# Attention layers of a two-block network: values weighted once per head slot, 256 columns, in place of once per query tile, 128 columns

## What is computed

```python
def _dilated_group(q, k, v, bias, window, dilation):
    ...
        logits = jnp.einsum('bqhd,bqkhd->bhqk', qb, kb, ...) * scale
        logits = logits + bias.astype(jnp.float32)[None, :, None, :]
        logits = jnp.where(valid[None, None], logits, NEG_INF)
        lse = jax.nn.logsumexp(logits, axis=-1)
        p = jnp.exp(logits - lse[..., None]).astype(vb.dtype)
        o = jnp.einsum('bhqk,bqkhd->bqhd', p, vb)
    ...
    wts = jax.nn.softmax(jnp.stack(lses, axis=0), axis=0)
    attn = jnp.einsum('gbsh,gbshd->bshd', wts, jnp.stack(outs, axis=0).astype(jnp.float32))
```

## Time and profile before

| | us |
|---|---|
| median of 3 runs | 1478.26 |
| lowest and highest | 1477.96, 1479.23 |
| profiled execution, its own time | 1477.93 |
| its span (first to last instruction) | 1476.1 |
| TensorE matmuls busy | 1463.0 (99%) |
| VectorE busy | 1131.1 (77%) |
| ScalarE busy | 801.4 (54%) |
| TensorE clock granted | 9 tenths or more (full) in each of 40 slices |

### The profile page before, as it was taken

One profiled execution on the slowest core, in us unless ns is written; L12 is line 12 of the kernel. 1 busy time (PEld: TensorE's weight loads), 2 busy tenths in 40 slices (PEclk: granted clock), 3 DMA queues, 4 the chain that ended last, 5 costly groups with the idle time before them and its releaser, 6 DMA issues.

```text
span 1476.1 us, 23650 instructions
## 1 busy us (share of the span) xinstructions
PE 1463.0 (99%) x10012; PEld 1311.9 (89%) x10012; DVE 1131.1 (77%) x1158; ACT 801.4 (54%) x931; POOL 470.2 (32%) x300
## 2 busy tenths in 40 slices
PE   9999999999999999999999999999999999999997
PEld 7889899888888889899888889998888899988886
DVE  7867776798787767776898667977997568789853
ACT  7444544665544444554666456356665446676642
POOL 3306200234698608001234744002444000134510
PEclk9999999999999999999999999999999999999999
DMA  8674455555556564466555444434554534355552
GB/s 288 228 222 175 143 172 176 196 181 190 185 206 250 182 246 143 143 252 240 186 186 200 158 162 168 140 119 172 195 180 182 188 130 161 143 194 179 191 186 79
DMA packets 48585, 269.93 MB, mean 183 GB/s; under 512 B 11488, under 2 KB 14816, under 8 KB 19552
## 3 DMA queue, kind: packets, MB, share of 16 engines
q1 hardware_dynamic: 48480, 268.43, 51.6%
HBM read 261.59 MB, written 6.82 MB: 182 GB/s over the span
## 4 chain that ended last, share of the span: by engine, by line
PE 96%; DVE 2%; ACT 1%; DMA 0%; issue 0%; SPq 0%; DVEq 0%; ACTq 0%
PE gemm L603 31%; PE gemm L576 23%; PE gemm L607 15%; PE aux L603 13%; PE aux L607 6%; PE aux L576 1%; PE aux L688 1%; ACT w_hi L1065 1%; PE aux L629 1%; DVE x_two L1518 0%; PE aux L810 0%; PE gemm L1006 0%; PE aux L690 0%; PE aux L665 0%; PE aux L678 0%; PE aux L670 0%
## 5 line engine op out<-in xcount | busy, mean ns | idle before, releaser
L1485 DVE TENSOR_TENSOR w_lo<-raw,w_hi 128x2048 fp32r<-128x2048 f32 (+3 forms) x244 | 588.4, 2415 | 131.8 <-ACT w_hi L1065 130.9
L1065 ACT ACTIVATE w_hi<-raw 128x2048 fp32r<-128x2048 f32 (+2 forms) x246 | 456.9, 1858 | 195.2 <-PE gemm L576 86.8
L603 PE MATMUL gemm<-x_two,w_hi 128*128 128x512 f32 x1184 | 373.4, 397 | 0.0
L607 PEld LDWEIGHTS gemm<-x_two,w_lo 128*128 128x128 f32 x1184 | 222.4, 188 | 52.6
L607 PE MATMUL gemm<-x_two,w_lo 128*128 128x256 f32 x1184 | 232.7, 278 | 0.0
L2215 POOL TENSOR_TENSOR tmp<-tmp 128x512 f32<-128x512 f32 (+1 forms) x29 | 43.8, 1510 | 466.9 <-ACT tmp L1092 453.3
L603 PEld LDWEIGHTS gemm<-x_two,w_hi 128*128 128x128 f32 x1184 | 180.4, 189 | 0.2
L2340 POOL TENSOR_TENSOR cv<-cv,rstd 128x512 f32<-128x512 f32 x44 | 112.0, 2545 | 210.6 <-ACT cv L1145 210.6
L603 PE MATMUL gemm<-y_two,w_hi 128*128 128x512 f32 x528 | 166.4, 396 | 0.0
L603 PE MATMUL aux<-x_two,w_hi 128*128 128x512 f32 x512 | 161.1, 396 | 1.0 <-DVE x_two L1518 1.0
L576 PE MATMUL gemm<-x_two,w_hi 128*128 128x256 f32 x672 | 123.2, 285 | 0.0
(11 more groups left out here) (388 smaller groups left out, 2675.5 us busy)
## 6 DMA issues: line engine op xcount, KB each, us to landing
raw<-in_weights SPq DMA_DIRECT2D x222, 1024.0 KB, 4.8
raw<-in_weights SPq DMA_DIRECT2D x16, 768.0 KB, 4.3
raw<-in_weights SPq DMA_DIRECT2D x8, 512.0 KB, 4.4
raw<-in_weights SPq DMA_DIRECT2D x4, 576.0 KB, 3.6
s_inputs<-s_made SPq DMA_DIRECT2D x1, 2048.0 KB, 8.9
s_outputs<-s_cw SPq DMA_DIRECT2D x1, 2048.0 KB, 10.8
s_v<-s_inputs SPq DMA_DIRECT2D x1, 2048.0 KB, 9.3
s_cw<-s_outputs SPq DMA_DIRECT2D x1, 2048.0 KB, 10.6
```

Source lines behind the costliest of these rows:

```text
L603: pe.matmul(dst[:, off:off + BANK], wh[:, wc, c0:c0 + P], both[:, xc, :, :], start=b.start and wc == 0, stop=b.stop and k + 2 == len(pairs ...
L607: mm = pe.matmul(dst[:, off:off + S], wl[:, wc, c0:c0 + P], both[:, xc, 0, :], start=False, stop=b.stop and k + 2 == len(pairs), skip_grou ...
L1065: me.give(act.activation(w_hi[i % SPL][:, 0:n], raw[i % RAW][:, 0:n], ACT.Copy), w_hi_ready)
L1485: me.give(v.tensor_tensor(w_lo[i % RAW][:, 0:n], raw[i % RAW][:, 0:n], w_hi[i % SPL][:, 0:n].bitcast(F32), ALU.subtract), w_lo_ready)
```

## The change

The values of a slot are weighted for both its query tiles at once. pt gets a place for each of the two tiles (ST = 2). `pv` is called with the slot, in the rounds 3, 5, 7 and 9, and in no other; it takes pt_ready twice. Its two products with va have 256 columns each, and four with vc of 64 columns follow, one for each class. ScalarE's copy and VectorE's subtraction take the 256 columns of a slot at once, in the same rounds. The copy to pt writes the tile's place, three pieces of 128. Products, sums and their order within an output are as before.

```diff
--- before.py
+++ after.py
@@ -266,7 +266,7 @@
         gate_p = tile("gate_p", r_gate, [P, DC, S])
         gate_a = tile("gate_a", r_gate + 8 * K, [P, DC, S])
         lg = tile("lg", r_att, [P, S + 2 * NC])
-        pt = tile("pt", r_att + 3 * K, [P, 3, P])
+        pt = tile("pt", r_att + 3 * K, [P, 3, ST, P])
         ao_h = tile("ao_h", r_att + 6 * K, [P, SLOTS, S], F32R)
         ao_l = tile("ao_l", r_att + 10 * K, [P, SLOTS, S], F32R)
 
@@ -678,17 +678,17 @@
                     mm = pe.transpose(A[:, 2 * BANK + k * P:2 * BANK + (k + 1) * P], lg[:, k * P:(k + 1) * P], ident)
                 me.give(mm, tr_ready)
 
-            def pv(u):
-                s, q = divmod(u, ST)
-                me.take(pt_ready)
-                if u:
+            def pv(s):
+                me.take(pt_ready, ST)
+                if s:
                     me.take(pv_read)
                 o, n, mm = 3 * BANK, slice(s * DH, (s + 1) * DH), None
                 for t in range(ST):
-                    pe.matmul(A[:, o:o + P], va[:, t, n], pt[:, t, :], start=t == 0, stop=False, skip_group_check=True)
-                for r in range(2):
-                    mm = pe.matmul(A[:, o + r * NC:o + (r + 1) * NC], vc[:, 2 * q + r, n], pt[:, 2, r * NC:(r + 1) * NC],
-                                   start=False, stop=r == 1, skip_group_check=True)
+                    pe.matmul(A[:, o:o + S], va[:, t, n], pt[:, t, :, :], start=t == 0, stop=False, skip_group_check=True)
+                for c in range(CLASS):
+                    q, r = divmod(c, 2)
+                    mm = pe.matmul(A[:, o + c * NC:o + (c + 1) * NC], vc[:, c, n], pt[:, 2, q, r * NC:(r + 1) * NC],
+                                   start=False, stop=c == CLASS - 1, skip_group_check=True)
                 me.give(mm, pv_ready)
 
             def table(k):
@@ -734,8 +734,8 @@
                         me.take(qkv_ready)
                     if j < 8:
                         scores(j)
-                    if 2 <= j:
-                        pv(j - 2)
+                    if j >= 3 and j % 2:
+                        pv((j - 3) // 2)
                     if 1 <= j < 9:
                         turn(j - 1)
                 me.take(scores_read)
@@ -1146,10 +1146,9 @@
                 y_half(PAIRS - 1)
                 then(first("down", n))
 
-            def pv_half(u):
-                s, q = divmod(u, ST)
+            def pv_half(s):
                 me.take(pv_ready)
-                me.give(act.activation(ao_h[:, s, q * P:(q + 1) * P], A[:, 3 * BANK:3 * BANK + P], ACT.Copy), pv_hi)
+                me.give(act.activation(ao_h[:, s, :], A[:, 3 * BANK:3 * BANK + S], ACT.Copy), pv_hi)
 
             def gate_of(j):
                 return (gate_p if j < 4 else gate_a)[:, 2 * (j % 4):2 * (j % 4) + 2, :]
@@ -1188,11 +1187,12 @@
                     split_next(ib)
                     if j >= 4:
                         gate(layer, j - 4)
-                    if 2 <= j:
-                        pv_half(j - 2)
+                    if j >= 3 and j % 2:
+                        pv_half((j - 3) // 2)
                     if 1 <= j < 9:
                         me.take(tr_ready)
-                        me.give(act.activation(pt.rearrange("p k n -> p (k n)"), A[:, 2 * BANK:2 * BANK + 3 * P], ACT.Copy),
+                        me.give(act.activation(pt[:, :, (j - 1) % ST, :],
+                                               A[:, 2 * BANK:2 * BANK + 3 * P].rearrange("p (k n) -> p k n", k=3), ACT.Copy),
                                 pt_ready)
                     if j < 8:
                         me.take(lg_ready)
@@ -1704,11 +1704,11 @@
                         lo(pl[:, :, :], tmp[:, :, :], ph[:, :, :])
                     else:
                         split_next(ib)
-                    if 2 <= j:
-                        s, q = divmod(j - 2, ST)
+                    if j >= 3 and j % 2:
+                        s = (j - 3) // 2
                         me.take(pv_hi)
-                        me.give(v.tensor_tensor(ao_l[:, s, q * P:(q + 1) * P], A[:, 3 * BANK:3 * BANK + P],
-                                                ao_h[:, s, q * P:(q + 1) * P].bitcast(F32), ALU.subtract), pv_read)
+                        me.give(v.tensor_tensor(ao_l[:, s, :], A[:, 3 * BANK:3 * BANK + S], ao_h[:, s, :].bitcast(F32),
+                                                ALU.subtract), pv_read)
                     if j < 8:
                         soft_a(j)
                     if j < 8:
```

## The result

The changed kernel takes 1486.3 us (median; 1484.24 to 1488.2) against 1478.17 us before: ratio 1.0053, 95% interval 1.0042 to 1.0065. It is slower by 8 us where 0.3 us faster was forecast.

The account below looks back on a forecast made before the run. TensorE was taken to bound the kernel. Per layer, three slots gain 0.03 us each, slot 3 loses 0.03, the pool gemm gains 0.09: 0.3 us over two layers, from 1478.26 to 1478.0 us; 8-in-10 range 1476.9 to 1479.3 us.

Parts of the forecast that it names:

- What bounds the kernel: Whole kernel: TensorE, busy 1463.0 of 1476.1 us; only its own time, or waits it is made to take, count.
- The rounds: Attention rounds 2 to 9: slots 0 to 2 gain 0.03 us each, slot 3 loses 0.03 us, per layer.
- The short rounds: Attention rounds 2, 4, 6, without values: 0.68 us from first head score to next gemm, 0.90 us shorter each.
- the long ones: Attention rounds 3, 5, 7, with a slot's values: 2.45 us from first head score to next gemm, 0.87 us more.
- the wide record: One 256-column f32 TensorE record of the values: 0.216 us, so four take 0.96 us, 0.42 us more.
- the weight load of the class values: Class values in long rounds: load-bound at 0.113 us each, no load saved; four more records cost 0.45 us.
- The pool gemm's wait: Pool gemm behind round 9, seventh chunk: TensorE's wait for VectorE's last subtraction goes, 0.09 us gained per layer.
- Beside TensorE: ScalarE's copy 0.38 us, VectorE's subtraction 0.41 us at 256 columns; sign: both engines with 1.2 us less each.
- Rival 1: Short rounds wait for the softmax, 0.6 us in rounds 2 and 4 of both layers: 1480.4 us; chance 0.05.
- Rival 3: Values' records at 256 columns take the 0.11 us of 128, eight slots gain 3.4 us: 1474.6 us; chance 0.02.
- the sum: Attention rounds and pool gemm: 0.15 us gained per layer, 0.3 us for two; from 0.5 slower to 0.8 faster.
- With 0.02 for what I don't see: Allowance for unseen effects in the odds for the whole kernel: faster 0.03, same 0.94, slower 0.03.

Follow-up runs that it names:

- after_again: The changed kernel run once more, unchanged, for a second trace: 1484.78 us, 1.0042 to the kernel before.
- before_m72: Kernel before, without the change, with 72 fewer TensorE instructions in the warm-up ahead of the first gemm: 1486.02 us, ratio 1.0048.
- after_p136: Changed kernel with 136 more TensorE instructions in the warm-up ahead of the first gemm: 1477.8 us, ratio 0.9997.
- after_slow72: Changed kernel with 72 TensorE instructions, 18 products of 128 columns at a gemm's pace, right ahead of the first burst: 1482.11 us, ratio 1.0026.
- after_split: Changed kernel, no padding, with groups 2 and 3 of the first burst moved between the two tiles of the gemm behind it: 1483.0 us, ratio 1.0029.
- after_mid72: Changed kernel with 72 TensorE instructions, 18 narrow products, put between the two bursts: 1484.77 us, ratio 1.0038.
- after_late72: Changed kernel with 72 TensorE instructions, 18 narrow products, put right ahead of the first burst: 1484.12 us, ratio 1.0040.
- after_m24: Changed kernel with 24 fewer TensorE instructions in the warm-up ahead of the first gemm: profiled execution 1480.04 us, the shortest of its six.
- after_m80: Changed kernel with 80 fewer TensorE instructions in the warm-up ahead of the first gemm; its measured time is not in the text given.

## Why the prediction was wrong

- *What bounds the kernel*: right. TensorE does, and each loss is one of its own.
- *The rounds*: right to 0.01 us. The short rounds took 0.69 us (0.68 forecast), the long ones 2.44 (2.45), the wide record 0.24 at most and 0.216 in series as in the earlier trace rows, and the weight load of the class values stayed the price of a 64-column record. Gained over both layers 0.25 us by the traces, 0.3 forecast.
- *The pool gemm's wait*: gone, 0.08 us a layer (0.09 forecast).
- *Beside TensorE*: ScalarE's wide copy took 0.375 us (0.38 forecast), VectorE's wide subtraction 0.419 us (0.41). So these two operations take 1.2 to 1.3 us less in all. The engines' busy time did not fall by that, as I had named as a sign: it is up by 2.6 us on VectorE, whose weight splits (w_lo) took 4.4 us more, and down by 0.3 us on ScalarE. I should have named the two lines in place of the totals.
- *Rival 1, late probabilities*: did not happen; no short round waits.
- *Rival 3, free columns*: did not happen; twice the columns took 0.216 us against 0.11.
- *The step that failed*: the sum put everything outside the attention rounds and the pool gemm at nothing, without a reason. "A difference of over 1 us in a stretch other than the attention rounds" stood at the end as a sign of error, but no term and no rival had a price for it; the runs showed 4.7 us at the two bursts from the place of TensorE's code, and 1.5 us near 1284 us. I counted the 32 records less as work saved and not as 72 instructions less of code. "With 0.02 for what I don't see" is where the result was. The trace of before had signs of it: the table of queues has q8 with 79 packets, TensorE's instructions divided by that are 257, and the burst's 512 instructions take 7.4 us, two pieces of code in a third of the time in which a gemm's code takes one (some 22 us). In it, too, 30 of the 79 code packets start right behind the close of a weight transfer. How much a late piece costs could not be read from it, since TensorE waited for none.

How the 8.1 us are made up: 3.3 us at the first burst, 1.4 us at the second and 1.5 us near 1284 us in the profiled execution, less 0.25 us in the rounds and 0.4 us of start on top, give its 6.3 us. That execution took 1484.24 us, the shortest of its kernel; the trace of after_again loses 4.8 us at the first burst, as its clock was low for 6.8 us there (before_m72 likewise, with 4.7 us). So the rest of the median is likely the same burst with a longer fall of the clock; the other executions have no trace that could show it.

A version that beats both did not come out: the change at a good place, after_p136, has 1477.8 us, and 0.9997 (0.9988 to 1.0007) is no difference that can be told.

## What to carry to other kernels

Count the instructions that a change takes from or adds to an engine, not only their time: behind it all code of that engine stands elsewhere against the ends of its pieces, and a kernel with dense bursts can lose several microseconds hundreds of microseconds further on. When a comparison shows a loss in a stretch that the edit does not touch and the wait is called "issue", shift the code by some dozens of instructions in a stretch that is idle anyway, and run the old kernel at the new places too, before you judge the edit. Padding works, but it holds only until the next edit; here the wait at the first burst also went when instructions at a gemm's pace stood ahead of it (after_slow72), or when it was cut in two halves of 256 (after_split), but each brought costs of its own. And look at what shares the DMA engines with the code: a burst that starts just ahead of a large transfer is the one whose code comes late.

## What the runs showed of the hardware

- TensorE's code comes in packets of 16 KB, 256 instructions. In a gemm's code a packet starts up to 40 instructions ahead of a piece's end. Some 2.3 to 2.6 us after the start of a late one TensorE went on with its piece. No two code packets started less than 3.34 us apart in any trace.
- A code packet that came due while a weight block of 1024 KB was under way (3.5 us) mostly started only when that was through: 585 of 1262 packets right behind a closing 4-byte packet, 32 in the middle of a block. In the burst (0.014 us an instruction) this made it 3.6 to 4.4 us late against the burst's start. At the second burst some packets came late with no block under way (960.66 us in after); why is not shown.
- The granted clock behind a standstill in such a burst: 1.2 GHz in place of 2.4 for 3.4 us in after (standstill 1.49 us) and after_mid72 (1.04 us), for 6.8 us in before_m72 (1.29 us), after_late72 (0.86 us) and after_again (1.3 us); no fall in after_m24 (1.03 us) and after_m80 (0.37 us). The length of the standstill alone doesn't tell which it will be.
